# Up projection with the weights stationary, and gate rows by a transpose and a broadcast load, in a two-block transformer kernel on one core

## The reference, cut to what matters

```python
mod = jax.nn.silu(c) @ w_ada[l] + b_ada[l]
sh1, sc1, g1, sh2, sc2, g2 = jnp.split(mod[:, None, :], 6, axis=-1)
...
x = x + g1 * (merged @ w_out[l])
h2 = rmsnorm(x, norm2_g[l]) * (1.0 + sc2) + sh2
x = x + g2 * conv_ffn(h2, w_up[l], conv_w[l], conv_b[l], w_down[l])

def conv_ffn(h, w_up, conv_w, conv_b, w_down):
    u = h @ w_up                      # (256, 2048) @ (2048, 2 * 5504)
    up = jnp.pad(u, ((0, 0), (CONV_WIDTH - 1, 0), (0, 0)))
    uc = conv_b
    for i in range(CONV_WIDTH):       # three taps along the tokens
        uc = uc + up[:, i:i + S] * conv_w[i]
    gate, val = jnp.split(uc, 2, axis=-1)
    return (jax.nn.silu(gate) * val) @ w_down
```

## Time and profile before

| | |
|---|---|
| median of 3 runs | 2297.28 us (2296.43 to 2298.26) |
| the profiled execution | 2297.32 us, its span 2295.5 us |
| granted TensorE clock, mean | 0.978 |
| busy, VectorE / ScalarE | 65% / 46% of the span |
| HBM read | 454.95 MB, 199 GB/s over the span |

### The profile page before, as it was taken

How to read it: one execution, slowest core, us unless ns; L and a number is a source line. 1 busy time by engine, 2 the same in 40 slices (tenths; PEclk the granted TensorE clock), 3 DMA queues, 4 the chain that set the end, 5 groups by cost and what they waited for, 6 DMA issues and landing times.

```text
span 2295.5 us, 27603 instructions
## 1 busy us (share of the span) xinstructions
PE 2162.0 (94%) x10218; PEld 1805.4 (79%) x10218; DVE 1493.9 (65%) x2227; ACT 1051.8 (46%) x1569; POOL 140.9 (6%) x131
## 2 busy tenths in 40 slices
PE   4899996698999999998999999999999999999997
PEld 4778885576788778887888888888778998888876
DVE  5958886697676767756557575545457755455565
ACT  2233335544454445444445454444554544434553
POOL 0100001011100000000002021000000210000100
PEclk9989998898999999999999999999999999999999
DMA  9959990096667666755555555544445555444443
GB/s 357 392 218 367 366 365 28 15 356 225 211 228 249 209 204 210 247 165 173 192 189 185 178 164 163 185 129 147 149 141 188 162 168 191 145 147 148 157 170 114
DMA packets 241612, 458.84 MB, mean 200 GB/s; under 512 B 12542, under 2 KB 164300, under 8 KB 240972
## 3 DMA queue, kind: packets, MB, share of 16 engines
q1 hardware_dynamic: 241484, 457.10, 58.3%
HBM read 454.95 MB, written 2.10 MB: 199 GB/s over the span
## 4 chain that ended last, share of the span: by engine, by line
PE 74%; DVE 5%; ACT 3%; issue 2%; POOL 0%; DMA 0%; DVEq 0%; ACTq 0%; SPq 0%; POOLq 0%
PE PS L285 22%; PE PS L292 22%; PE PS L287 22%; PE PS L1079 2%; PE PS L1022 2%; DVE WLO L276 1%; PE PS L1199 1%; ACT WHI L268 1%; PE PS L1087 1%; DVE SPARE L370 1%; DVE BIG L1480 1%; PE PS L1094 0%; PE PS L1096 0%; PE PS L1095 0%; PE PS L926 0%
## 5 line engine op out<-in xcount | busy, mean ns | idle before, releaser
L285 PE MATMUL PS<-WHI,HH 128*128 128x512 f32 (+4 forms) x2680 | 1061.5, 396 | 35.3 <-ACT WHI L268 16.3
L276 DVE TENSOR_TENSOR WLO<-RAWT,WHI 128x1024 fp32r<-128x1024 f32 (+4 forms) x694 | 830.5, 1204 | 355.8 <-ACT WHI L268 355.7
L287 PE MATMUL PS<-WHI,HLO 128*128 128x512 f32 (+4 forms) x2680 | 1039.6, 388 | 2.0 <-issue 2.0
L268 ACT ACTIVATE WHI<-RAWT 128x1024 fp32r<-128x1024 f32 (+4 forms) x694 | 691.9, 1015 | 378.1 <-PE PS L292 315.2
L292 PE MATMUL PS<-WLO,HH 128*128 128x512 f32 (+4 forms) x2680 | 714.2, 389 | 3.1 <-DVE WLO L276 3.1
L285 PEld LDWEIGHTS PS<-WHI,HH 128*128 128x128 f32 x2680 | 508.3, 190 | 145.0 <-issue 25.4
L292 PEld LDWEIGHTS PS<-WLO,HH 128*128 128x128 f32 x2680 | 505.6, 189 | 103.2 <-DVE WLO L276 4.7
L287 PEld LDWEIGHTS PS<-WHI,HLO 128*128 128x128 f32 x2680 | 509.2, 190 | 96.0 <-issue 3.3
L370 DVE SCALAR_TENSOR_TENSOR AD<-AD,SM 128x1024 f32<-128x1024 f32 x83 | 110.4, 1330 | 10.1 <-DMA AD<-w_ada 8.2
L1124 ACT ACTIVATE WK<-PS 128x384 f32<-128x384 f32 x48 | 23.4, 487 | 194.4 <-PE PS L1087 194.4
L723 ACT ACTIVATE HH<-BIG 128x256 fp32r<-128x256 f32 x118 | 48.6, 412 | 108.3 <-PE PS L292 107.2
(11 more groups left out here) (277 smaller groups left out, 1478.2 us busy)
## 6 DMA issues: line engine op xcount, KB each, us to landing
RAWT<-w_up SPq DMA_DIRECT2D x168, 512.0 KB, 4.8
AD<-w_ada SPq DMA_DIRECT2D x152, 512.0 KB, 5.8
RAWT<-w_out SPq DMA_DIRECT2D x96, 512.0 KB, 4.5
RAWT<-w_in SPq DMA_DIRECT2D x48, 1024.0 KB, 5.1
RAWT<-w_down SPq DMA_DIRECT2D x86, 512.0 KB, 4.6
RAWT<-w_in SPq DMA_DIRECT2D x44, 992.0 KB, 7.9
RAWT<-w_in SPq DMA_DIRECT2D x40, 924.0 KB, 4.9
BIG<-w_ada SPq DMA_DIRECT2D x40, 512.0 KB, 11.1
```

The source lines that it names most:

```text
L268: act.activation(WHI[:, (q % HL) * GR:(q % HL) * GR + size], r, ACT.Copy).then_inc(S("hi_done"), 1)
L276: dve.tensor_tensor(WLO[:, (q % HL) * GR:(q % HL) * GR + size], r, h.bitcast(F32), ALU.subtract)\
L285: pe.matmul(o, lh, wh, start=first and bank not in seen, stop=False)
L287: pe.matmul(o, ll, wh, start=False, stop=False)
```

## The change

The up projection gets its own TensorE loop, `up_pe`. It holds 128 x 128 blocks of the weights stationary and moves all 256 tokens past them, so results come out with columns on partitions: four tiles of 256 columns in two banks. A group is 2 blocks x 4 tiles x 3 terms = 24 matmuls of 256 columns. The copies to `U` and the transposes are gone; the taps read the banks of the chunk itself, the first tap at group 4 in place of 6, and TensorE waits before a chunk until the taps have left its banks (`ff_conv`). Before the down projection it waits for the last chunk's taps.

Each gate row is made by one transpose to 16 x 128, one copy, one store of 8 KB to device memory and two loads of 4 KB broadcast to all partitions. For g1 transpose and copy are in the input projection's chunks 9 and 10 and the loads behind the index scores; for g2 they are in the last chunk of the up projection, and SyncE's store and loads stand ahead of the final norm row. One buffer of the index scores (`SC`) moves by 102 columns, out of the way of g1's row. The diagonals, the eight products and their copies go.

```diff
+        def ffn_tile(par, t):
+            return PS[:, 2 * ((up.c0 + par) % 2) + t // 2, (t % 2) * T:(t % 2 + 1) * T]
+
+        def up_pe(pe, it, par, nt, stat=None, after=None, ada=None):
+            cn = it * 2 + par
+            for s in range(up.spc):
+                gs, reg = slot_of(up, it, par, s)
+                for j in range(2):
+                    q, gi = 2 * gs + j, 2 * s + j
+                    if gi == 0:
+                        ge(pe, S("ff_conv"), cn - 1)
...
+                    tiles_ = [(k, t) for k in range(2) for t in range(2 * nt)]
...
+                    pe.wait_ge(S("hi_done"), reg * 2 + (q + 1))
+                    for k, t in tiles_:
+                        kt, o = 2 * gi + k, ffn_tile(par, t)
+                        pe.matmul(o, WHI[:, wt[k, t]], HHv[:, kt, :], start=kt == 0 and t % 2 == 0, stop=False)
+                        pe.matmul(o, WHI[:, wt[k, t]], HLv[:, kt, :], start=False, stop=False)
+                    pe.wait_ge(S("lo_done"), reg * 2 + (q + 1))
+                    for k, t in tiles_:
+                        kt = 2 * gi + k
+                        mm = pe.matmul(ffn_tile(par, t), WLO[:, wt[k, t]], HHv[:, kt, :], start=False,
+                                       stop=kt == KT - 1 and t % 2 == 1)
+                    mm.then_inc(S("mm_done"), 1)
...
-        def ffn_turn(pe, cn, nt):
...
-            for t in range(2 * nt):
-                for h in range(2):
-                    mm = pe.transpose(ffn_tile(t)[:, h * P:(h + 1) * P], U[:, h, t * P:(t + 1) * P], ident)
-            mm.then_inc(S("ff_turn"), 1)
...
-            act.wait_ge(S("ff_turn"), cn + 1)
+            act.wait_ge(S("mm_done"), it * (4 * up.spc) + 2 * (up.g0 + up.spc * (par + 1)))
...
-                    eng.matmul(PS[:, 6, :], ones, dg, start=True, stop=True).then_inc(S("gr_mm"), 1)
...
+        def gate_row_out(eng, who, z):
+            if who == "pe":
+                eng.wait_ge(S("ada_out"), 12 if z else 6)
+                eng.transpose(PS[0:KT, 6, 0:P], MODC[:, GATE_AT[z]:GATE_AT[z] + KT], ident).then_inc(S("gr_turn"), 1)
+            elif who == "act":
+                eng.wait_ge(S("gr_turn"), z + 1)
+                eng.activation(GTMP, PS[0:KT, 6, 0:P], ACT.Copy).then_inc(S("gr_tmp"), 1)
+            else:
+                eng.wait_ge(S("gr_tmp"), z + 1)
+                eng.dma_start(gate_dram[z].ap(), GTMP).then_inc(S("gr_dram"), 16)
+                eng.wait_ge(S("gr_dram"), 16 * (z + 1))
+
+        def gate_row_in(sp, z, c, dst):
+            row = gate_dram[z].ap().rearrange("(c k) p -> c (k p)", c=2)[c:c + 1, :]
+            sp.dma_start(dst, row.broadcast_to((P, 1024))).then_inc(S("gr_row"), 16)
...
             w_in_rest(sp, "sp")
+            gate_row_out(sp, "sp", 0)
+            sp.wait_ge(S("ix_used"), len(IXG))
+            for half in range(2):
+                gate_row_in(sp, 0, half, GROW[:, half * 1024:(half + 1) * 1024])
             kout(sp, "sp", "w_out", w_out[0], 16, None, ty, ada=8)
             run_up(sp, "sp", None)
 
             sp.wait_ge(S("ada_red"), 12)
+            gate_row_out(sp, "sp", 1)
+            for half in range(2):
+                gate_row_in(sp, 1, half, GROW2[half])
             sp.wait_ge(S("rel_w"), 16)
...
-            pe.wait_ge(S("ev_act"), up.c0 + UPN)
-            pe.wait_ge(S("ev_dve"), up.c0 + UPN)
-
-            def banks_up(e):
-                e.wait_ge(S("ff_conv"), UPN)
-                e.wait_ge(S("gr_row"), 8)
+            pe.wait_ge(S("ff_conv"), UPN)
```

More of the change, by code:

```diff
@@ L98, in build_program @@
     rel_dram = nc.dram_tensor("rel_table", (4, REL), F32, kind="Internal")
+    gate_dram = [nc.dram_tensor(f"gate_row{z}", (KT, P), F32, kind="Internal") for z in range(2)]
     ctx = ExitStack()
@@ L232, in build_program @@
         two_loads = set()
-        for name, slots, chunks in (("w_in", 44, 11), ("w_out", 16, 0), ("w_up", 88, 22), ("w_down", FT, 0)):
+        for name, slots, chunks in (("w_in", 44, 11), ("w_out", 16, 0), ("w_up", 88, 0), ("w_down", FT, 0)):
             place[name] = (g, cc)
@@ L580, in w_in_rest @@
                 elif who == "pe":
-                    chunk_pe(eng, ph, it, par, ada="w_in")
+                    chunk_pe(eng, ph, it, par, ada="w_in", after={5: lambda e: gate_row_out(e, who, 0)} if cn == 9 else None)
                 else:
@@ L1242, in build_program @@
         GROW2 = [AD[:, 0:1024], WK[:, 2048:3072]]
[L1244 to L1259, removed]
-                    eng.matmul(PS[:, 6, :], ones, dg, start=True, stop=True).then_inc(S("gr_mm"), 1)
[L1261 to L1265, removed]
+        GATE_AT = (32, 80)
@@ L1267, in build_program, with pair @@
+        def gate_row_in(sp, z, c, dst):
+            row = gate_dram[z].ap().rearrange("(c k) p -> c (k p)", c=2)[c:c + 1, :]
+            sp.dma_start(dst, row.broadcast_to((P, 1024))).then_inc(S("gr_row"), 16)
         UPN = 22
         def run_up(eng, who, prep, stat=None):
[L1271 to L1277, removed]
+            def pair(it, pars, ada=None, stat=None, gate=False):
@@ L1315, in run_up @@
             pair(9, (0, 1))
-            pair(10, (0, 1), beside=gate2_rows(who))
+            pair(10, (0, 1), gate=True)
             if who == "act":
-                chunk_out(eng, up, 10, 1, 0, n=256, dst=U[:, 0, 0:256])
-                ffn_act_tap2(eng, 21, 1)
+                ffn_act_tap2(eng, 10, 1, 1)
                 ffn_act_silu(eng, 21, 1)
@@ L1991, in _ @@
             turn(act, "act", merged1_turns(0), ty)
-            softmax_heads(act, "act", dsa_jobs(), ty, beside=gate1_rows("act"))
+            softmax_heads(act, "act", dsa_jobs(), ty)
             act.wait_ge(S("sm_o_out"), 8)
@@ L2140, in _ @@
             turn(dve, "dve", merged1_turns(0), ty)
-            softmax_heads(dve, "dve", dsa_jobs(), ty, chain, beside=gate1_rows("dve"))
-            dve.wait_ge(S("gr_row"), 4)
+            softmax_heads(dve, "dve", dsa_jobs(), ty, chain)
             dve.wait_ge(S("sm_o_out"), 8)
@@ L2297, in _ @@
             turned(pe, ty)
-            softmax_heads(pe, "pe", dsa_jobs(), ty, beside=gate1_rows("pe"))
+            softmax_heads(pe, "pe", dsa_jobs(), ty)
             pe.wait_ge(S("sm_o_out"), 8)
             merged_norm1(pe, "pe", 1, ty)
-            pe.wait_ge(S("gr_row"), 4)
             turn(pe, "pe", merged1_turns(1), ty)
```

80 lines of the change are left out of this document (33 added, 47 removed).

## The result

| | before | after |
|---|---|---|
| median | 2297.8 us (4 runs, 2296.4 to 2299.8) | 2271.8 us (4 runs, 2268.5 to 2275.0) |
| ratio | | 0.9886, interval 0.9869 to 0.9903 |
| profiled execution, its span | 2297.32, 2295.5 | 2273.24, 2271.4 |
| granted clock, mean | 0.978 | 0.977 |

What follows compares the result with a forecast made beforehand. TensorE, busy for 94% of the span, was taken as the bound. Terms -5.2 + 0.1 - 2.6 - 2.7 - 1.2 + 2.3 - 2.8 + 0.15 = -12.0 us took 2297.28 to 2285.3, range 2279.0 to 2291.0.

Steps and rivals of the forecast that it cites:

- the pitch: Up projection, full chunks: 24 half-width matmuls take 2.825 us, a chunk 22.60 against 22.86; -5.2 us over twenty chunks.
- Rival (d): Up projection: half-width matmuls at exactly half the pitch, chunk 21.99, -17.4 in place of -5.2; 2273.1 us, 2%.
- Banks and taps: Up projection: taps read the banks directly and free them long before TensorE needs them; costed at nothing.
- Second gate row and last chunk: End of up projection: three gate products gone from the twenty-first chunk, -2.6 us; last chunk 14.64 to 11.95, -2.7.
- The products' -2.6: Twenty-first up chunk: three products of ones with a diagonal leave TensorE, 0.86 us each; -2.6 us.
- Joint: Between up and down projection: tap starts sooner, -1.2 us, but the down weights come late, +2.3.
- The tap: Joint to the down projection: the tap starts right after the last up matmul; -1.2 us.
- The queue: Before the down projection: gate row's write and loads delay the first down weights to T+17.8, T the last chunk's start; +2.3 us.
- Attention gate row: Attention softmax: four gate products leave TensorE's chain, -2.8 us; turning the row in the input projection adds 0.15.
- Loop's jump: Up projection's chunk loop: the jump's 6.5 us of waits and half clock stays; zero, bounds -4 and +3.
- Instruction supply, rival (c): Up projection: TensorE is not fed with instructions, 18 extra pieces at 2.0 us idle, +36; 2321 us, 7%.

Runs made afterwards that it cites:

- halves: The kernel before, with each 512-column up matmul of the full chunks split into two of 256 columns, tokens still stationary; 2311.3 us, ratio 1.0052.
- halves_lone: halves with the eight transposes of a chunk cut to one, so its result is not the reference's; 2292.8 us, one run.
- early_rows: The changed kernel with the second gate row turned two chunks earlier and small loads put between the weight slots of chunks 20 and 21; 2268.0 us, ratio 0.9873.
- overlap: early_rows with another bank for the last chunk and that chunk's taps, silu and gating moved into the down projection; 2264.5 us, ratio 0.9864.
- g1_only: The kernel before with only the attention half's gate row made the new way; 2291.9 us, ratio 0.9979.
- no_reduce_again: The changed kernel without the modulation's small float32 reductions on TensorE in the chunk loop, run a second time for its trace; 2265.3 us, one run.

## Why the prediction was wrong, point by point

**The step that failed is the pitch.** "I take 2.825 for 24 in one group ... so a chunk is 8 x 2.825 = 22.60" took the half-width matmul's price from the last chunk of the kernel before. The instruction was the same in width and count, but not in which operand is stationary, and I took that for indifferent. halves and halves_lone show that the row was right for its own arrangement. The changed kernel's matmuls have 2.72 as well, and had it in four groups of five. With it a chunk is 21.76, the twenty chunks give 20 x 1.10 = 22.0, less 34 long groups x 0.107 = 3.6: 18.4 in place of 5.2. The first down matmul comes 12.6 us earlier than the sum said, and this term is 13.2 of that, the others 0.6 the other way, because their own misses nearly cancel: the joint came 1.0 better and the last chunk 0.3, the attention 1.75 worse and the rest 0.1. The bound of 2 us that I put on this term came from the third digit of one row, so it covered the reading and not the question whether the row was the right one. Rival (d), half the width at half the time, gave 2273.1 and 2%. It came out nearest, and I had set it aside for the rows of the half-sized chunk, which are of the other arrangement. Its mechanism isn't the measured one either: half of the 512-column pitch is 2.747 for a group, and the groups take 2.72 or 2.83. What was right: that this term is a small difference of two large ones, and that each nanosecond is 3.8 us; it was off by 4.4 ns for most of the stage.

By the Trainium skill, "TensorE: Matmul & The Clock Gate", section Back-to-back issue gap, which gives its formula for an isolated matmul, the two forms differ by 31 ns a group to the disadvantage of the halves, an estimate. The traces don't agree. The kernel before has 12 x 0.2289 = 2.747, and against that 2.72 is 27 ns to the advantage of the halves, 2.827 is 80 ns to their disadvantage.

**Banks and taps.** Right: no wait for the taps' banks shows in the full chunks.

**Second gate row and last chunk.** The last chunk took 11.6 us, from 1041.65 to 1053.3, against 11.95; -3.0 in place of -2.7. The products' -2.6 in the chunk before it fits: from the end of the output projection to 1041.65 the trace gains 20.8, which is 18.4 and 2.6 less 0.2.

**Joint.** Net +1.1 was forecast, +0.1 came. The tap saved what it should. The queue was the right mechanism and a term too large: the write landed at T+3.3 (forecast 4.1, bounds 3.5 to 6, so faster than the lower one; 1.40 us for 8 KB against 1.9 of the row of c; the same write for the first gate row, at 331 us, took 5.95), and the first down weights at T+16.4 (forecast 17.8). ScalarE was ready at T+15.3 (15.4), so it waited 1.17 us and not 2.3; early_rows confirms that by taking 1.27 off the gap.

**Attention gate row.** The steps became 1.66 and 1.80 us (forecast 1.80), and the stage, from its first transposes to the first high part of the output projection, 31.7 us against 34.7, -3.0 where -2.8 was forecast. But that stage begins 2.6 us later: 0.3 of it lies in the input projection and most in the stretch from 400 to 420, at a granted clock of 0.76 against 0.84. Over eleven traces with the new row the stage takes 31.3 to 33.3 us and over three without it 34.7 to 36.6, and it begins at 415.6 to 421.1 against 417.4 to 418.9. In this pair of traces, then, most of what the products cost is given back ahead of them, with a lower clock that I had left out, and -0.9 is left at the end of the output projection. But that is this pair and not the change: the clock from 400 to 420 is 0.76 in halves too, which has the old row, and 0.84 in overlap, which has the new one. Over all fourteen traces the output projection's first high part starts at 451.1 on average with the new row and at 453.4 without (three traces), 2.3 earlier where 2.65 was forecast. So the term was about right, and the pair shows it too small. What makes the clock lower in some traces isn't shown.

**Loop's jump.** Right: one wait of 4.17 us now where there were 2.29 and 2.03, and half clock behind it, 6.7 us in all against 6.5. That one wait came where there were two, at the same cost, was luck: g1_only shows that the jump can also cost 3.7 us less.

**Instruction supply, rival (c).** It didn't come: 14 packets more in the instruction queue (98 against 84), and no idle time put down to issue in the up projection away from the jump. By the Trainium skill, "Runtime: NRT & Kernel Launch", section Instruction fetch mechanics, the crossing from block to block is mostly hidden; this trace agrees.

The terms as measured: -18.4 (full chunks), -2.6 + 0.2 (gate products, rest), -3.0 (last chunk), +0.1 (joint), -0.9 (attention and output projection) make -24.6 at the first down matmul, of which 0.5 is lost behind it. The -0.9 holds for this pair of traces alone.

## What to carry to other kernels

The price of a matmul is not only its number of columns. A row is evidence for a new arrangement only where stationary and moving operand play the same parts. Where they don't, the range should take in half the time of a matmul of twice the width, and a little less. When a stage is nothing but matmuls back to back, read the distance of starts over the whole stage, not at one place: it can have two values, each held for hundreds of matmuls, and a handful of small float32 products or transposes can move it from one to the other. Work of ScalarE and VectorE that TensorE would otherwise wait for between two projections (taps, silu) belongs behind the first groups of the next projection, not in front of them.

## What the runs showed of the hardware

- With 256 columns moving past stationary weights there are two pitches, 0.1133 and 0.1178 us, at the same granted clock of 1.00. The down projection's 512-column matmuls, with the tokens stationary, show two as well, 0.2333 and 0.2289 us. Here are third terms of the changed kernel, then of no_reduce_again, 2.80 against 2.74 us for 12:

```profile
1102.07 0.93 PE PS L292 x4
...
1104.87 0.93 PE PS L292 x4
```

```profile
1101.30 0.91 PE PS L292 x4
...
1104.04 0.91 PE PS L292 x4
```

- In these traces a pitch is held for as long as nothing else comes between: where it changed there stood small plain float32 products, a plain float32 transpose, or a wait of TensorE, and each of these also left it unchanged somewhere (the reductions only with the tokens stationary, in halves and halves_lone). The difference is 4.4 ns a matmul at either width (0.107/24, 0.053/12). It makes two runs of one program differ by up to 17 us (15.6 between the two traced). The mechanism stays open.
- A loop's jump costs 3.7 to 4.5 us of idle time in thirteen of the fourteen traces, with a stretch at half clock behind it, and 2.2 us at full clock in g1_only, without any change in the loop.
- With the weights stationary each matmul has a weight load of its own (12048 for 12048). Its record lasts 0.19 us, and the matmuls still start every 0.113 us.
- A write of 8 KB to device memory landed after 1.40 us in all ten traces that have it behind the loop. For the first gate row, at about 330 us, it took 5.1 to 6.7 us.
